# One-hot rows for expert 0, four banks for the output projection, and permuted token slots in a transformer block with a mixture of experts

## The chip, the cores and the metric

The kernel runs on one core of one Trainium2 chip. The core has five engines with an instruction queue each: TensorE (PE in the profile, with its weight loads as PEld), VectorE (DVE), ScalarE (ACT), GpSimd (POOL) and SyncE (SP, which here only issues DMAs). They share an SBUF of 128 partitions; matmul results land in eight banks of PSUM, each 128 partitions by 512 float32 numbers. Sixteen DMA engines move data between HBM and SBUF. The engines run side by side and wait for each other only by semaphores.

The metric is the device time of one execution in microseconds (us), here the median of three timed runs. Everything is float32.

## The reference, cut to what matters

```python
# 128 context tokens and 256 latent tokens, D_MODEL = 1024; N_EXPERTS = 32 in 4 groups, D_EXPERT = 256
def trunk_layer(x, mod, lp, latent, ctx_k, ctx_v, s0_fwd, s0_bwd):
    sh1, sc1, g1, sh2, sc2, g2 = jnp.split(mod, 6, axis=-1)
    h = ln_plain(x) * (1 + sc1) + sh1
    ...                                       # attention and gated linear attention from h @ w_in
    merged = gates[:, :, 0] * (attn @ lp['w_br_attn']) + gates[:, :, 1] * (gla @ lp['w_br_gla'])
    x = ln_affine(DEEPNORM_ALPHA * x + g1 * (merged @ lp['w_out']), lp['ln1_g'], lp['ln1_b'])
    h2 = ln_plain(x) * (1 + sc2) + sh2
    x = ln_affine(DEEPNORM_ALPHA * x + g2 * hier_moe(h2, lp), lp['ln2_g'], lp['ln2_b'])

def hier_moe(h, lp):
    lg = (t @ lp['router_group_w'] + lp['router_group_b'])      # the best of 4 groups
    le = (t @ lp['router_expert_w'] + lp['router_expert_b'])    # the best 2 of its 8 experts
    ...
    for e in range(N_EXPERTS):
        hid = jax.nn.silu(t @ lp['exp_w_gate'][e]) * (t @ lp['exp_w_up'][e])
        y = y + comb[:, e:e + 1] * (hid @ lp['exp_w_down'][e])
```

Each of the 384 tokens goes to 2 of the 32 experts, so 768 pairs of token and expert are computed. An expert's three weights are 1 MB each.

## The kernel before, in words

The tokens are three tiles of 128 (tiles 0 and 1 latent, tile 2 context). The program is written out by hand for each engine; PE's order of work is the order of the code. Where a result goes to a PSUM bank, a small table (`Banks`) hands out the banks of a ring in turn: `claim` makes PE wait until the last user of the bank was read, `wait_full` makes a reader wait for the matmuls, `was_read` gives it back.

The first part (to about 343 us) computes modulation, projections, both mixers and the branch projections; the change doesn't touch it, except that one group of loads is issued there. What comes then, in order:

- **Output projection** (PE L1779): for each tile and each half of the 1024 columns, 8 matmuls over 512 columns, six groups in all, that take banks 0 and 1 in turn. DVE (L1073 to the `norm_affine` calls) multiplies each half by the gate, adds the scaled residual (L1077) and takes statistics of the half (L837); with both halves it does the affine layer norm with `ln1_g` and `ln1_b` (aggregate L844, L846, L854), where GpSimd computes the power -0.5 (L689), and at once the second, modulated norm (L837, L844, L846, L851), whose last instructions write the rows `h2` of the tile and raise `h2_ready`. `ln1` is loaded by ACT (L1431) into a piece of Y that the branch outputs occupied until then.
- GpSimd stores each tile's `h2` to HBM (L727) as half rows of 2 KB, two for each token.
- **Router**: PE transposes `h2` (L1646), ACT copies the transposes (L1435), PE multiplies by the router's weights (L1796); DVE picks group and two experts (L1089 to L1121, `both_ready`). PE computes each token's rank among the tokens of its expert by triangular matmuls (L1804, L1806). Between these, `keep_busy(n)` has PE do n idle matmuls of 512 columns (L1523).
- **Index tables**: DVE picks the ranks out (L1132, L1139) and compares each with a row of constants `iota_rows` (L1147), PE multiplies the six one-hot tables (L1823), and DVE writes the indices `gidx` and `sidx` (L1151, L1152). An expert has 64 slots; column j of `iota_rows` holds the rank that slot j takes. In the kernel before that is j itself. A slot is two rows (partition j and partition 64 + j) of 2 KB, the halves of a token. Unused slots get an index out of bounds and move nothing but a few bytes.
- **Experts** (32, one after the other): GpSimd gathers an expert's rows from HBM (L732), PE transposes them (L1839), ACT copies (L1446), PE multiplies by gate and up weights (L1865, two groups of 64 output partitions side by side), ACT and DVE make the hidden values (L1464, L1188), PE transposes and multiplies by the down weights (L1898, L1874), DVE scales (L1206), GpSimd scatters to HBM (L737). Six weight buffers are filled by SP: the first ones from 315 us on, as their space comes free (down of expert 1 and all of 2 behind the last group of the output projection, 4 behind `h2_ready`, the up weights of 5 when `h2` is stored and transposed). From expert 6 on, gate and up weights are asked for when the gate and up products of the expert six before are done (`gu_full`), the first time at expert 0.
- The last two experts' rows are added by PE; the others' sums are read back from HBM (SP L664), added and normed.

SP's and ACT's loads each keep their order on one queue, GpSimd's on a third.

## Time and profile before

| | us |
|---|---|
| median of three timed runs | 677.2 (675.61 to 678.33) |
| the profiled execution's own time | 672.36 |
| its span, first to last instruction | 670.6 |
| PE busy | 621.0 (93%) |
| DVE busy | 265.9 |
| GpSimd busy | 115.6 |
| ACT busy | 106.6 |

The profiled execution is 4.8 us under the median of the timed ones. "Busy" for PE counts the time from issue to a modelled end, and the idle matmuls of `keep_busy` too. The row of digits for DMA gives the busy share of the sixteen DMA engines in 40 slices of 16.8 us: it is 9 from the 27th slice to the 38th, that is from about 436 to 637 us. The stretch before, from 352 to 436 us, is 5, 0, 9, 7, 8.

### The profile page before, as it was taken

The page shows a single profiled execution, that of the slowest core. Times are in us where ns is not written, and L with a number is a line of the kernel's source. Part 1 is how long each engine was busy: PE and PEld are TensorE (multiplying, and loading weights), DVE is VectorE, ACT ScalarE, POOL GpSimd, SP SyncE. Part 2 cuts the span into 40 slices and gives each one's busy share as a digit, 9 for nine tenths or more (in the row PEclk, how much of TensorE's full clock was granted, in tenths as well). Part 3 has the DMA queues.
Part 4 walks back from the last instruction along what each step waited for, and adds up shares of the span by engine and source line. Part 5 has one row for each costly group of instructions (what it writes and reads, how often), then busy time and mean ns, then how long its engine had stood idle before and what let it go on. Part 6 is the DMA issues. An engine that isn't in the chain of part 4 may idle for free.

```text
span 670.6 us, 8592 instructions
## 1 busy us (share of the span) xinstructions
PE 621.0 (93%) x3403; PEld 344.4 (51%) x3403; DVE 265.9 (40%) x593; ACT 106.6 (16%) x222; POOL 115.6 (17%) x114
## 2 busy tenths in 40 slices
PE   6999999999999999999999998999999887788994
PEld 3553355546455556555544464665566544444541
DVE  4322533145445544302224865334333232222347
ACT  2001553110032222330000021111111111111000
POOL 4000000010300000000001323334334222221102
PEclk9999999999999999999999999999999999988998
DMA  9998737344131130409995097899999999999862
GB/s 336 376 332 289 251 127 251 126 158 157 24 127 58 69 126 1 126 0 317 372 402 223 38 359 296 333 420 416 413 414 417 413 417 414 415 416 419 352 241 94
DMA packets 56200, 176.65 MB, mean 263 GB/s; under 512 B 10644, under 2 KB 12724, under 8 KB 44512
## 3 DMA queue, kind: packets, MB, share of 16 engines
q1 hardware_dynamic: 39264, 143.34, 55.4%
q10 hardware_dynamic: 11152, 24.47, 10.4%
q0 software_dynamic: 5744, 8.28, 3.5%
q8 instruction: 28, 0.46, 0.3%
q14 instruction: 12, 0.10, 0.0%
HBM read 174.58 MB, written 11.96 MB: 278 GB/s over the span
## 4 chain that ended last, share of the span: by engine, by line
PE 60%; DMA 22%; DVE 8%; issue 2%; POOL 2%; ACT 2%; SPq 2%; ACTq 0%; DVEq 0%; POOLq 0%
PE bank L1592 13%; PE bank L1865 11%; DMA X<-exp_w_up 8%; PE bank L1581 7%; PE bank L1766 6%; PE bank L1874 5%; DMA Y<-exp_w_up 4%; PE bank L1545 3%; DMA Y<-ln_b 3%; DMA X<-w_ada 2%; PE bank L1505 2%; DMA Y<-w_ada 2%; POOL rstd L689 2%; PE bank L1839 2%; PE bank L1733 1%
## 5 line engine op out<-in xcount | busy, mean ns | idle before, releaser
L1865 PE MATMUL bank<-X,Y 128*64 128x256 f32 x672 | 82.0, 395 | 11.8 <-DMA X<-exp_w_up 10.8
L1592 PE MATMUL bank<-Y,W 128*128 128x384 f32 x256 | 86.6, 492 | 0.0
L1865 PEld LDWEIGHTS bank<-X,Y 128*64 128x64 f32 x672 | 50.7, 137 | 48.0 <-DMA X<-exp_w_up 18.0
L689 POOL TENSOR_TENSOR rstd<-ss,cst 128x1 f32<-128x1 f32 (+3 forms) x21 | 22.6, 1075 | 295.7 <-DVE ss L822 295.7
L1592 PEld LDWEIGHTS bank<-Y,W 128*128 128x128 f32 x256 | 47.4, 190 | 36.0 <-issue 5.6
L1581 PE MATMUL bank<-W,Y 128*128 128x512 f32 x144 | 64.0, 597 | 0.0
L732 POOL DMA_INDIRECT Y<-h_rows,gidx x32 | 41.4, 1293 | 92.9 <-PE bank L1839 88.4
L1192 DVE COPY abias<-bank 128x128 f32<-128x128 f32 x32 | 9.3, 292 | 117.1 <-PE bank L1898 117.1
L1865 PE MATMUL bank<-W,Y 128*64 128x256 f32 (+1 forms) x320 | 37.2, 346 | 7.5 <-DMA W<-exp_w_up 3.9
L737 POOL DMA_INDIRECT pair_rows<-PTr,sidx x32 | 32.9, 1029 | 61.2 <-DVE PTr L1206 60.6
L1779 PE MATMUL bank<-X,Y 128*128 128x512 f32 x96 | 41.7, 594 | 1.3 <-issue 1.0
L1874 PE MATMUL bank<-X,abias 128*64 128x512 f32 x176 | 42.6, 603 | 0.0
L1581 PEld LDWEIGHTS bank<-W,Y 128*128 128x128 f32 x144 | 26.7, 190 | 30.9 <-issue 30.7
L1766 PE MATMUL bank<-Y,W 128*128 128x384 f32 x128 | 41.8, 487 | 0.8 <-PE bank L1592 0.5
L1464 ACT ACTIVATE abias<-bank 128x128 f32<-128x128 f32 x32 | 8.9, 278 | 186.9 <-PE bank L1865 180.2
L1545 PE MATMUL bank<-W,Y 128*128 128x288 f32 (+1 forms) x96 | 33.8, 504 | 0.7 <-DVE Y L919 0.7
L1865 PEld LDWEIGHTS bank<-W,Y 128*64 128x64 f32 x320 | 23.2, 139 | 20.7 <-DMA W<-exp_w_up 5.7
L1766 PEld LDWEIGHTS bank<-Y,W 128*128 128x128 f32 x128 | 24.2, 190 | 18.4 <-issue 2.0
L1206 DVE TENSOR_TENSOR PTr<-bank,abias 128x512 f32<-128x512 f32 x32 | 22.1, 692 | 25.6 <-PE bank L1874 25.6
L1779 PEld LDWEIGHTS bank<-X,Y 128*128 128x128 f32 x96 | 18.1, 190 | 24.7 <-issue 24.7
L1523 PE MATMUL bank<-cst 128*128 128x512 f32 x48 | 25.0, 660 | 5.0 <-DMA cst<-consts 5.0
L1062 DVE TENSOR_TENSOR Y<-bank,Y 128x384 f32<-128x384 f32 x16 | 8.9, 558 | 46.9 <-PE bank L1766 46.9
(232 smaller groups left out, 723.2 us busy)
## 6 DMA issues: line engine op xcount, KB each, us to landing
X<-exp_w_gate SPq DMA_DIRECT2D x22, 1024.0 KB, 22.1
X<-exp_w_up SPq DMA_DIRECT2D x22, 1024.0 KB, 26.1
X<-exp_w_down SPq DMA_DIRECT2D x22, 1024.0 KB, 26.6
Y<-w_ada ACTq DMA_DIRECT2D x16, 1024.0 KB, 8.2
W<-w_in SPq DMA_DIRECT2D x7, 2048.0 KB, 9.0
W<-exp_w_gate SPq DMA_DIRECT2D x10, 1024.0 KB, 22.1
W<-exp_w_up SPq DMA_DIRECT2D x5, 1024.0 KB, 26.7
W<-exp_w_down SPq DMA_DIRECT2D x5, 1024.0 KB, 29.7
```

Of the source, the lines that this page charges most:

```text
L689: nc.gpsimd.tensor_tensor(rstd[:, 0:n], ss[:, 0:n], const("mhalf", 0, n), ALU.pow)\
L732: pool.indirect_dma_start(G[:, n % NSLOT, :], None, h2_d, bass.IndirectOffsetOnAxis(ap=gidx[:, n:n + 1], axis=0), bounds_check=2 * TOKENS ...
L737: pool.indirect_dma_start(yp_d, bass.IndirectOffsetOnAxis(ap=sidx[:, n:n + 1], axis=0), Yo[:, n % NY, :], None, bounds_check=2 * TOPK * TO ...
L1206: V.tensor_tensor(Yo[:, n % NY, :], banks[6][:, :], gw, ALU.mult).then_inc(S["y_ready"], 1)
L1523: mm(banks[6][:, :], ident, cst[:, 0:HALF], start=True, stop=True)
L1545: ins = mm(bank[:, 0:cols], hT[:, i, k, :], w[:, k, :], start=k == 0, stop=k == KT - 1)
L1581: ins = mm(bank[:, :], hT[:, i, k, :], w[:, k, :], start=k == 0, stop=k == KT - 1)
L1592: ins = mm(bank[:, 0:TOKENS], w[:, k, c * P:(c + 1) * P], hT[:, :, k, :], start=k == 0, stop=k == KT - 1)
L1766: ins = mm(bank[:, 0:TOKENS], w[:, m, k, (c % 4) * P:(c % 4 + 1) * P], src[:, :, k, :], start=k == 0, stop=k == 3)
L1779: ins = mm(bank[:, :], mT[:, i, k, :], w[:, k, :], start=k == 0, stop=k == KT - 1)
L1865: ins = mm(bank[hh * 64:hh * 64 + 64, a:b], x_[:, c, h * 64:h * 64 + 64], rhs(hh), start=k == 0 and a == 0, stop=k == KT - 1, skip_group_c ...
L1874: ins = mm(banks[6][o * 64:o * 64 + 64, :], hT_[:, hh * 64:hh * 64 + 64], wd[hh][:, o * HALF:(o + 1) * HALF], start=hh == 0, stop=hh == 1, ...
```

## The change: what it does

1. **ln1 earlier, g2 later.** ACT loads `ln1_g` and `ln1_b` into PTr right behind the modulation rows; the four small loads of the second gate, which went there, come behind `h2_ready` of the last tile. The intermediate of the second norm goes to Y instead of PTr.
2. **Four banks, last piece halved.** The output projection takes banks 0, 1, 4 and 5 in turn, and the last group (tile 2, second half) becomes two of 256 columns; DVE handles these in two pieces, and takes tile 2's statistics in four pieces of 256 columns.
3. **Expert 0's rows by one-hot products.** DVE makes three one-hot tables of 64 slots from the rank matrix; PE multiplies them with `h2` in SBUF (6 matmuls into bank 1), ACT copies. Expert 0 is not gathered from HBM any more. The idle matmuls are 6 behind the router (5 before), 1 behind the ranks (2), and none before expert 0's transposes (4). SP's load of expert 5's up weights waits for these products in place of the last transposes.
4. **Permuted slots.** Column j of `iota_rows` holds another rank: ranks 0 to 7 go to slots 0, 4, 8, ... 28, ranks 8 to 15 to slots 1, 5, 9, ..., and so on in each block of 32 slots.

```diff
-    put("iota_rows", np.repeat((np.arange(P) % SLOT_ROWS)[None], P, 0))
+    at = np.arange(P) % SLOT_ROWS
+    put("iota_rows", np.repeat((at // 32 * 32 + at % 4 * 8 + at % 32 // 4)[None], P, 0))
...
-FILL_NORM, FILL_ROUTER, FILL_RANK, FILL_GATHER = 4, 5, 2, 4
+FILL_NORM, FILL_ROUTER, FILL_RANK = 4, 6, 1
...
+WO_COLS = {(n, i): slice(n * HALF, (n + 1) * HALF) for i in range(TILES) for n in range(2)}
+WO_COLS[1, LAST_TILE] = slice(HALF, HALF + HALF // 2)
+WO_COLS[2, LAST_TILE] = slice(HALF + HALF // 2, 2 * HALF)
...
-        ln1 = lambda j: Y1[:, j, 0, :]
-        ln2 = ln1
+        ln1 = lambda j: PTr[:, 2 * j:2 * j + 2, :].rearrange("p a n -> p (a n)")
+        ln2 = lambda j: Y1[:, j, 0, :]
...
+        last = Banks((0, 1, 4, 5), banks, full, read, last_jobs(), uses)
+        expert0 = Banks((1,), banks, full, read, [("rows",)], uses)
...
-            side.wait_full(sp, "hT", TILES - 1, 1)
+            expert0.wait_full(sp, "rows")
             load_part(sp, "exp_w_up", 1, PARTED, PARTED, ew_in[PARTED])
...
-            for n in range(NSLOT):
+            for n in range(1, NSLOT):
                 gather_rows(n)
...
+                    for c in range(cols.start, cols.stop, chunk):
+                        ins = V.bn_stats(stats[:, c // chunk, :], x1(i)[:, c:c + chunk])
+                    step(ins)
...
             bank = side.wait_full(dve, "rank")
+            for i in range(TILES):
+                ins = V.tensor_scalar(first_slots[:, i, :], const("iota_rows", 0, SLOT_ROWS), bank[:, i * NE:i * NE + 1],
+                                      both[:, i, 0:1], ALU.is_equal, ALU.mult)
+            ins.then_inc(S["onehot_ready"], FIRST_SLOTS)
...
+            bank = expert0.wait_full(act, "rows")
+            expert0.was_read(A_(G[:, 0, :], bank[:, :], ACT.Copy), "rows")
...
+            pe.wait_ge(S["onehot_ready"], FIRST_SLOTS)
+            bank = expert0.claim(pe, "rows")
+            for i in range(TILES):
+                for h in range(2):
+                    ins = mm(bank[h * SLOT_ROWS:(h + 1) * SLOT_ROWS, :], first_slots[:, i, :],
+                             xr(i)[:, h * HALF:(h + 1) * HALF], start=i == 0, stop=i == TILES - 1, skip_group_check=True)
+            expert0.filled(ins, "rows")
...
             index_tables(0)
-            keep_busy(FILL_GATHER)
             next_tokens(0)
```

VectorE, tile 2 of the output projection, from the gate's product to the last row of `h2`. Before:

```order
L1073 TENSOR_TENSOR Y<-bank,X 128x512
L1077 SCALAR_TENSOR_TENSOR Y<-Y 128x512
L837 BN_STATS stats<-Y 128x6
L1073 TENSOR_TENSOR Y<-bank,X 128x512
L1077 SCALAR_TENSOR_TENSOR Y<-Y 128x512
L837 BN_STATS stats<-Y 128x6
L844 BN_AGGR mv<-stats 128x2
```

The same place with the change:

```order
L1092 TENSOR_TENSOR Y<-bank,X 128x512
L1097 SCALAR_TENSOR_TENSOR Y<-Y 128x512
L1100 BN_STATS stats<-Y 128x6 x2
L1092 TENSOR_TENSOR Y<-bank,X 128x256
L1097 SCALAR_TENSOR_TENSOR Y<-Y 128x256
L1100 BN_STATS stats<-Y 128x6
L1092 TENSOR_TENSOR Y<-bank,X 128x256
L1097 SCALAR_TENSOR_TENSOR Y<-Y 128x256
L1100 BN_STATS stats<-Y 128x6
L862 BN_AGGR mv<-stats 128x2
```

Three instructions of 512 columns became six of 256, and there are four statistics in place of two.

TensorE, from the idle matmuls behind the router to expert 0's gate and up products. Before:

```order
L1523 MATMUL bank<-cst 128x512 x5
L1804 MATMUL bank<-both,cst 128x96
L1806 MATMUL bank<-both,cst 128x64
L1806 MATMUL bank<-both,cst 128x32
L1812 MATMUL bank<-both,cst 128x32 x3
L1523 MATMUL bank<-cst 128x512 x2
L1820 MATMUL bank<-cst 128x64
L1823 MATMUL bank<-wgate,abias 128x64 x4
L1823 MATMUL bank<-wgate,zbias 128x64 x2
L1523 MATMUL bank<-cst 128x512 x4
L1839 MATMUL bank<-cst,Y 128x128 x4
L1865 MATMUL bank<-X,Y 64x256 x16
```

With the change:

```order
L1550 MATMUL bank<-cst 128x512 x6
L1832 MATMUL bank<-both,cst 128x96
L1834 MATMUL bank<-both,cst 128x64
L1834 MATMUL bank<-both,cst 128x32
L1840 MATMUL bank<-both,cst 128x32 x3
L1550 MATMUL bank<-cst 128x512
L1851 MATMUL bank<-Y,abias 64x512 x6
L1856 MATMUL bank<-cst 128x64
L1859 MATMUL bank<-wgate,abias 128x64 x4
L1859 MATMUL bank<-wgate,zbias 128x64 x2
L1875 MATMUL bank<-cst,Y 128x128 x4
L1901 MATMUL bank<-X,Y 64x256 x16
```

The six products of expert 0's rows (L1851) stand ahead of the index tables, and the four idle matmuls behind the tables are gone.

ScalarE, its loads around the output projection. Before:

```order
L1418 DMA X<-modulation_rows 128x1024 x6
L1422 DMA PTr<-modulation_rows 64x512 x4
L1428 DMA Y<-x_sample 128x1024 x2
L1428 DMA Y<-x_prompt 128x1024
L1431 DMA Y<-ln_g 128x1024
L1431 DMA Y<-ln_b 128x1024
L1435 ACTIVATE Y<-bank 128x512 x6
L1439 DMA Y<-ln_g 128x1024
L1439 DMA Y<-ln_b 128x1024
```

With the change:

```order
L1444 DMA X<-modulation_rows 128x1024 x6
L1447 DMA PTr<-ln_g 128x1024
L1447 DMA PTr<-ln_b 128x1024
L1451 DMA Y<-x_sample 128x1024 x2
L1451 DMA Y<-x_prompt 128x1024
L1455 ACTIVATE Y<-bank 128x512 x6
L1460 DMA PTr<-modulation_rows 64x512 x4
L1464 DMA Y<-ln_g 128x1024
L1464 DMA Y<-ln_b 128x1024
```

The first pair of `ln` loads moved ahead of the `x` loads, and the four loads of the second gate moved behind the evictions.

## Rows read from the trace of the kernel before

**Rows 1.** The page's first line: span and instructions
```profile
span 670.6 us, 8592 instructions
```

**Rows 2.** Stretches: length, busy of five engines, granted clock, DMA share, GB/s
```profile
409.00:411.00 2.00, 1.40 (x13) 1.30 (x12) 0.65 (x4) 0.00 (x0) 0.00 (x0) 1.00 1.04 432
...
413.00:422.50 9.50, 7.97 (x56) 5.31 (x54) 0.52 (x2) 2.75 (x4) 6.71 (x8) 1.00 0.38 106
422.50:530.00 107.50, 106.89 (x864) 66.73 (x863) 40.52 (x91) 14.88 (x34) 39.58 (x34) 1.00 1.01 412
532.41:614.86 82.45, 67.91 (x483) 36.27 (x483) 22.60 (x50) 8.75 (x20) 21.85 (x19) 0.96 1.02 416
...
630.00:634.00 4.00, 4.00 (x19) 1.47 (x17) 2.03 (x4) 0.00 (x0) 1.26 (x1) 1.00 0.80 328
```

**Rows 3.** Timeline of PE, gate and up products of experts 18 and 28: start, length
```profile
532.41 3.84 PE L1865 MATMUL bank<-X,Y 128*64 128x256 f32 x32 [2.09 <-DMA X<-exp_w_up]
...
614.86 3.85 PE L1865 MATMUL bank<-X,Y 128*64 128x256 f32 x32
```

**Rows 4.** The chain of waits, its last part
```profile
594.08 28.50 DMA Y<-exp_w_up
```

**Rows 5.** Timeline of SP: the first load that expert 0 releases
```profile
420.90 0.33 SPq L485 DMA_DIRECT2D X<-exp_w_gate  x1
```

**Rows 6.** Timeline of DVE in the output projection
```profile
359.00 0.69 DVE L837 BATCH_NORM_STATS2 stats<-Y 128x6 f32<-128x512 f32 x1
363.02 0.21 DVE L844 BATCH_NORM_AGGREGATE mv<-stats 128x2 f32<-128x12 f32 x1 [3.33 <-DMA Y<-ln_b]
...
373.52 0.69 DVE L1073 TENSOR_TENSOR Y<-bank,X 128x512 f32<-128x512 f32 x1
...
384.01 0.69 DVE L1073 TENSOR_TENSOR Y<-bank,X 128x512 f32<-128x512 f32 x1
...
388.42 0.21 DVE L844 BATCH_NORM_AGGREGATE mv<-stats 128x2 f32<-128x12 f32 x1
...
395.28 1.41 DVE L851 SCALAR_TENSOR_TENSOR Y<-PTr,rstd,X 128x512 f32<-128x512 f32 x2 [0.52 <-POOL rstd L689]
```

**Rows 7.** Timeline of PE from the output projection to expert 0
```profile
343.43 27.71 PE L1779 MATMUL bank<-X,Y 128*128 128x512 f32 x64 [0.30 <-PE bank L1766]
372.13 13.97 PE L1779 MATMUL bank<-X,Y 128*128 128x512 f32 x32 [0.99 <-issue]
...
392.32 3.68 PE L1523 MATMUL bank<-cst 128*128 128x512 f32 x8
396.75 1.23 PE L1646 MATMUL bank<-cst,Y 128*128 128x128 f32 x8 [0.75 <-DVE Y L851]
...
400.00 4.54 PE L1523 MATMUL bank<-cst 128*128 128x512 f32 x10
405.61 0.46 PE L1804 MATMUL bank<-both,cst 128*128 128x96 f32 x2 [1.07 <-DVE both L1121]
...
409.70 1.10 PE L1823 MATMUL bank<-wgate,abias 128*128 128x64 f32 x8 [0.60 <-DVE zbias L1147]
...
415.50 0.75 PE L1839 MATMUL bank<-cst,Y 128*128 128x128 f32 x4 [0.76 <-DMA Y<-h_rows,gidx]
417.02 3.85 PE L1865 MATMUL bank<-X,Y 128*64 128x256 f32 x32 [0.78 <-ACT Y L1446]
```

**Rows 8.** Groups by form: busy, mean ns
```profile
L879 DVE TENSOR_TENSOR Y<-X,cst 128x256 f32<-128x256 f32 x4 | 1.7, 425 | 0.1
L879 DVE TENSOR_TENSOR Y<-X,cst 128x64 f32<-128x64 f32 x4 | 0.9, 226 | 0.1
```

**Rows 9.** Timeline of PE: one expert's down products, four matmuls
```profile
427.31 1.94 PE L1874 MATMUL bank<-X,abias 128*64 128x512 f32 x8
```

**Rows 10.** Timeline of GpSimd: the first gather; then the page's queue row of GpSimd's DMAs
```profile
412.34 1.11 POOL L732 DMA_INDIRECT Y<-h_rows,gidx  x1 [3.62 <-DVE sidx L1152]
...
q0 software_dynamic: 5744, 8.28, 3.5%
```

More of the change, by code:

```diff
@@ L619, in _ @@
             load_part(sp, "exp_w_gate", 0, PARTED, PARTED, ew_in[PARTED])
-            for n in range(2):
-                main.wait_full(sp, "wo", n, TILES - 1)
+            for n in range(3):
+                last.wait_full(sp, "wo", n, LAST_TILE)
             load_down(sp, 1, 1, ed_in[1])
@@ L1791, in _ @@
                 if i == 0:
-                    bank = main.claim(pe, "router")
+                    bank = last.claim(pe, "router")
                 for g in range(2):
@@ L1879, in next_tokens @@
             def next_tokens(n):
[L1880 removed]
+                if n:
+                    pe.wait_ge(g_in[n % NSLOT], (n // NSLOT + (n % NSLOT > 0)) * 16)
+                else:
+                    expert0.wait_read(pe, "rows")
                 if n:
```

87 lines of the change are left out of this document (46 added, 41 removed).

## The prediction, made before the changed kernel ran

> **What bounds the kernel now.** I read the page first, then the stretches, because PE's busy share of 93% is an average over stages with different limits. From 422.50 to 614.86 us the sixteen DMA engines are busy without a break, at a share of 1.01 to 1.02 and 412 to 416 GB/s [rows 2]. The same span of time holds the experts. In its second part PE waits for the up weights of nearly every expert [rows 3]: from 532.41 to 614.86 us lie ten experts, so 8.25 us each, while the gate and up products themselves take 3.84 us. The chain of waits ends in the same place, in a load of up weights that took 28.50 us from issue to landing, because it stood behind others [rows 4]. So the end of the kernel is set by two things: when the unbroken stream of weights starts, and how fast the slowest DMA engine works through it. Behind the last of these loads (594.08 + 28.50 = 622.6) come 48 us up to the end of the span at 670.6 [rows 1]: PE, scatter, read-back and norms, which the change leaves alone.
>
> The start of the stream is a release: the first load of it is issued at 420.90 us [rows 5], when expert 0's gate and up products (417.02 + 3.85) are done [rows 7]. From 413.00 to 422.50 us the DMA engines are busy only 0.38 of the time [rows 2]. What brings expert 0 forward closes this hole, and all that follows moves with it. Expert 0 itself hangs on a serial chain: output projection, two norms for each tile, router, ranks, tables, gather, transposes.
>
> **The change part by part.** All times are of the profiled execution.
>
> *ln1 earlier.* Tile 0's statistics end at 359.00 + 0.69 = 359.7, but the aggregate starts at 363.02, behind ln_b's landing [rows 6]. With the load issued ahead of the x loads, behind the modulation rows, that wait of 3.3 us goes. The 0.5 MB more in that earlier stretch meets w_out, which isn't needed before 343.43; I count nothing. What is late next is PE: the fourth group ends 343.43 + 27.71 = 371.1 [rows 7], so DVE takes tile 1's second half at about 371.4 in place of 373.52 [rows 6]. That is 2.1 us at this point.
>
> *Four banks, last piece halved.* With two banks PE lost 0.99 us at 372.13 waiting for a bank [rows 7]; that goes, and the last group ends near 385.0 in place of 386.1. DVE begins tile 2 at 384.01 - 2.1 = 381.9. Its work there was 388.42 - 384.01 = 4.41 us. Now the first half costs 0.69 + 0.04 + 0.69 + 0.04 and two statistics of 256 columns, each taken at 0.43 as the 256-column product of another line [rows 8], 2.3 us in all; the two quarters cost six instructions of 0.43 and a gap of 0.03, 2.8 us. The sum is 5.1, so 0.7 more than before, and it ends at 387.0. PE's last quarter is there by 385.0, so DVE never waits: the halving hides nothing any more and costs 0.7. If 256 columns cost half of 512 (0.35), the loss is 0.2; by 0.5 each it is 1.2. `h2_ready` of tile 2 comes 2.1 - 0.7 = 1.4 us sooner. PE's idle matmuls ahead of its transposes end at 396.0 - 1.0 = 395.0, against `h2` at 396.69 - 1.4 = 395.3 [rows 6, 7]: no new wait.
>
> *One more idle matmul behind the router.* Ten half matmuls took 4.54 us, twelve take 5.45; PE was idle for 1.07 us behind them [rows 7]. 0.9 fits; nothing.
>
> *The one-hot tables on DVE.* Three instructions of 64 columns ahead of the rank products, at 0.226 us [rows 8] or less: 0.65 us, all on the path to the tables, since DVE has no gap there. Two scalars, one from PSUM, could make it 1.2. Behind them wait ranks, tables, indices and the gathers for experts 1 to 3.
>
> *Expert 0's rows on PE.* Four matmuls of this shape (64 output partitions, 512 columns, the two halves of a bank in turn) took 1.94 us [rows 9], so six take 2.9 us. PE starts them after one idle matmul, 0.9 us behind the counts' last product. In us from the ranks' first product, which moves from 405.61 to 404.2: products of ranks and counts 1.4, idle matmul 0.9, rows 2.9, which gives 409.4. The tables are ready at 409.7 - 1.4 + 0.65 = 408.9, so they wait 0.5 us for PE, and the index tables end near 411.3. ACT's copy of the rows lies beside them. Transposes run at 411.3, and by the same 1.52 us as before (417.02 - 415.50 [rows 7]) gate and up start at 412.85. Before it was 417.02. **Expert 0 is 4.2 us sooner**: 1.4 from the norms, minus 0.65 for the tables, minus 0.75 for the rows that the tables wait behind (0.5, and the opening product that no longer runs early), plus 4.2 for the gather, its wait and issue (from 411.3, the tables' end before as now, to 415.50). The gather for expert 1 starts near 412.4, where the one for expert 0 did [rows 10], and lands 3.1 us later if it does as that one did, ahead of 416.7, when PE wants it. If the six products didn't run in pairs, they would cost 12 x 0.43 = 5.2 us and the gain would be 1.9; without the tables' delays at all it would be 5.5.
>
> *The stream.* The first release moves from 420.90 to 416.7. But the gathers and scatters that ran in the hole (0.38 of 9.5 us, that is 3.6 us of all engines) have only 5.3 us of it left; those of about 1.8 us fall away or still fit, one gather is gone, and some 0.7 us of work moves into the full stretch. The stream ends **3.5 us sooner** by this alone.
>
> *The slots.* A DMA can be no faster than its slowest engine. Three weights are 3.15 MB; at the 432 GB/s of a stretch with hardly anything else [rows 2] they take 7.3 us, at 420 they take 7.5, and the experts come every 8.25 us. So the engine that sets the pace spends 0.75 to 0.95 us per expert on gathers and scatters. The mean engine spends less: 8.28 MB in 3.5% of 670.6 us [rows 10] are 2.8 us per MB, and 24 tokens (768 over 32) gathered and scattered are 0.2 MB, so 0.5 us. And from 630.00 to 634.00, after the last load, the share is 0.80 [rows 2]: some engines are done and others have a backlog. That is skew, and the permutation acts on it. How rows go to engines no row tells. If neighbouring pairs of rows go to the sixteen engines in turn, the engine with the first pair always has four rows in each transfer, 8 x 0.08 = 0.64 us per expert and more for experts with over 32 tokens: near the measured excess. Counting the tokens of each expert in the reference's router (6 to 59) by this rule, with 0.16 us for a pair of rows (4 KB at 432/16 = 27 GB/s), half of it for a single row and 0.01 for none, the fullest engine has 22.9 us of gathers and scatters before and 21.1 after, as the even pairs fill with ranks 0 to 15 and the odd ones with 16 to 31. I take **1.7 us sooner** up to the last load that matters, with bounds of 0 and, for a perfect spread, 22.9 - 14.6 = 8.3.
>
> Here a rule speaks for another result. The Trainium skill, DMA: Bandwidth & Descriptors, section "Why a DMA increments its semaphore by 16 and not by 1", says that GpSimd's direct copies may give each engine a block of one sixteenth of the partitions, so 8 rows in a row. By that rule the first engine would have 71 us of small transfers before and 54 after, a rate of 8.6 us per expert before. The trace's 8.25 doesn't agree, so I give it a small chance below.
>
> **The sum.** -3.5 - 1.7 = -5.2 us. Against the profiled execution: 672.36 - 5.2 = 667.2. The median of the runs shown lies 4.8 above that execution; I carry the difference over: 677.2 - 5.2 = 672.0 us. What a measurement of this kernel can tell from no change is about 0.5%, 3.4 us.
>
> **The rivals.**
> - *Only the start moves.* The permutation changes nothing, as when the pace is set by something else than the fullest engine. -3.5: 673.7. For it: the share of 1.02 shows no idle engine; against it: 8.25 us per expert against 7.8 by the mean engine's load. Chance 0.22.
> - *The early gain is lost before the first release.* The gather for expert 1, or the load of the second gate (now behind `h2_ready`, sharing the engines with 7 MB of weights), comes late and expert 0 or 1 stands; or the six products don't pair. The first release gains 1 to 2 us: 675.5. Chance 0.14.
> - *Blocks of eight rows.* The rule above: 17 us less on the fullest engine, of which the release order gives back part, as PE then sets the pace in many experts: I take about half, and the earlier start with it, -11, so 666. Chance 0.06.
> - *Slower: single rows go to engines in turn.* Then slots 0, 4, 8, ... hit four engines only. The place is the stream from expert 6 on. With 0.08 us a row the fullest engine goes from 37.4 to 44.3 us: +6.9 - 3.5 = +3.4, so 680.6. It decides once the four engines' extra rows exceed what the earlier start gave, 3.5 us. For it: the same skew of sixteen us between engines. Against it: 37.4 us over 28.5 experts (27 gathers and 30 scatters) are 1.3 us per expert, more than the excess of 0.95. Chance 0.06.
> - The forecast has the rest, 0.52, with its own range of 669.5 to 674.
>
> **How the numbers follow.** Faster by over 0.5% means under 673.8: nine tenths of the forecast (0.47), half of the first rival (0.11), all of the third (0.06), 0.64. Slower by over 0.5%: the fourth rival's half and a little of the second and of the scatter between runs, 0.06. The rest, 0.30, is within 0.5%. The range reaches from between the forecast and the third rival, 668.3, to 676.5, which holds the first and most of the second.
>
> **What would show it.** In the changed profile: no wait for ln at the first aggregate, which starts near 359.7; tile 2's `h2` near 395.2; the six products in about 2.9 us; expert 0's gate and up near 412.9 and SP's first refill near 416.7; the DMA share full from about 418 on; 8.15 to 8.2 us per expert in the second part; the last waited load landing near 617.4. The forecast is wrong if the first refill isn't at least 3 us sooner, or if it is and the last waited load isn't.

## The result, and the profile of the changed kernel

The changed kernel took 664.07 us (median of 4 executions, 663.80 to 667.03) against 676.52 (675.61 to 678.33) on the same chip: a ratio of 0.9826, with a 95% interval of 0.9806 to 0.9845. That is 12.5 us less; 5.2 less were forecast, and 664.07 lies below the range. Two more series of runs gave 665.33 and 664.64 for the same kernel (ratios 0.9863 [0.9839, 0.9886] and 0.983 [0.9809, 0.9852]). The median of all 15 executions is 664.64, and that is the changed kernel's time below where a kernel of another series is compared with it. The series ran on different chips: the kernel before took 676.9 us beside experiments 1 to 4, 675.5 beside 5 to 8, 674.5 beside 9 to 14 and 676.1 beside 15 and 16. So a difference of medians from two series carries up to some 2.5 us; the ratios, each against the kernel before in its own series, and the landings in the traces are the better measures.

The profiled execution is the longest of its four, 667.03 us. The page's span, TensorE clock, DMA shares and GpSimd queue, to be read against [rows 1, 10]:

```profile
span 665.3 us, 8643 instructions
...
PEclk9999999999999999999999999999999999999898
DMA  9997737345030330308995089999999999999952
...
q0 software_dynamic: 5664, 8.14, 3.5%
```

The first digit 8 near the end of the clock's row is a fall to half clock (1.2 GHz in place of 2.4) at 618.7 us, which the other three executions don't show in their time (spans of 662.0 to 662.4).

The output projection and the norms on DVE (start us, length, instruction, idle time before it in brackets), which answer to [rows 6]:

```profile
360.17 0.21 DVE L862 BATCH_NORM_AGGREGATE mv<-stats 128x2 f32<-128x12 f32 x1
...
371.72 0.69 DVE L1092 TENSOR_TENSOR Y<-bank,X 128x512 f32<-128x512 f32 x1 [1.10 <-PE bank L1807]
...
382.21 0.69 DVE L1092 TENSOR_TENSOR Y<-bank,X 128x512 f32<-128x512 f32 x1
...
384.45 0.42 DVE L1092 TENSOR_TENSOR Y<-bank,X 128x256 f32<-128x256 f32 x1
...
387.20 0.27 DVE L862 BATCH_NORM_AGGREGATE mv<-stats 128x2 f32<-128x24 f32 x1
...
394.13 1.41 DVE L869 SCALAR_TENSOR_TENSOR Y<-Y,rstd,X 128x512 f32<-128x512 f32 x2 [0.52 <-POOL rstd L706]
...
405.62 0.77 DVE L1154 TENSOR_SCALAR abias<-cst,bank,both 128x64 f32<-128x64 f32 x3
```

The wait for ln_b is gone, PE is next (1.10 us), and the three one-hot tables take 0.77. On PE, from the idle matmuls to the second expert, against [rows 7]:

```profile
405.81 1.10 PE L1550 MATMUL bank<-cst 128*128 128x512 f32 x2
...
409.84 1.06 PE L1859 MATMUL bank<-wgate,abias 128*128 128x64 f32 x8
...
411.18 0.68 PE L1875 MATMUL bank<-cst,Y 128*128 128x128 f32 x4
412.64 3.85 PE L1901 MATMUL bank<-X,Y 128*64 128x256 f32 x32 [0.78 <-ACT Y L1471]
416.78 0.75 PE L1875 MATMUL bank<-cst,Y 128*128 128x128 f32 x4 [0.29 <-DMA Y<-h_rows,gidx]
```

Expert 0 no longer waits for a gather; expert 1 does, for 0.29 us. Its gather was issued at 412.43, so it was used 4.3 us behind its issue. The stretches (length, busy time of five engines, granted clock, DMA share, GB/s) and the last load in the chain of waits, against [rows 2, 4]:

```profile
413.00:417.00 4.00, 3.71 (x33) 2.51 (x30) 0.60 (x3) 1.01 (x2) 3.08 (x4) 1.00 0.72 258
...
526.80:606.84 80.04, 64.73 (x483) 34.88 (x483) 23.27 (x50) 8.75 (x20) 22.34 (x19) 1.00 1.02 416
```

```profile
586.47 28.04 DMA Y<-exp_w_up
```

From 526.80 to 606.84 lie ten experts that wait for up weights: 8.00 us each, against 8.25. The last waited load lands at 586.47 + 28.04 = 614.5, against 622.6: 8.1 us sooner, of which expert 0's earlier start (412.64 against 417.02) explains at most 4.4. The first load that expert 0 releases is issued at 416.79, against 420.90 in [rows 5]. From there to the last waited landing it is 197.7 us, against 201.7 before.

### The profile page after: what moved, and what is told of

Same layout as the page of the kernel before. It is cut to its first block, busy times and chain, and to the rows that moved or that the text cites. A ratio compares the mean times of both kernels' runs of the same rounds, so it can differ in the third digit from the quotient of the medians.

```text
span 665.3 us, 8643 instructions
## 1 busy us (share of the span) xinstructions
PE 619.1 (93%) x3423; PEld 348.1 (52%) x3423; DVE 266.9 (40%) x600; ACT 107.2 (16%) x223; POOL 114.5 (17%) x113
## 4 chain that ended last, share of the span: by engine, by line
PE 70%; DMA 15%; DVE 8%; issue 3%; ACT 2%; POOL 1%; SPq 0%; ACTq 0%; DVEq 0%; POOLq 0%
PE bank L1619 13%; PE bank L1901 12%; PE bank L1608 7%; PE bank L1793 6%; PE bank L1910 5%; DMA Y<-exp_w_up 4%; PE bank L1807 4%; DMA X<-exp_w_up 4%; DMA W<-exp_w_up 4%; PE bank L1572 3%; PE bank L1532 2%; DMA Y<-w_ada 2%; PE bank L1875 2%; POOL rstd L706 1%; PE bank L1760 1%
## 5 line engine op out<-in xcount | busy, mean ns | idle before, releaser
L1901 PE MATMUL bank<-X,Y 128*64 128x256 f32 x672 | 80.6, 389 | 12.4 <-DMA X<-exp_w_up 11.4
L706 POOL TENSOR_TENSOR rstd<-ss,cst 128x1 f32<-128x1 f32 (+3 forms) x21 | 22.6, 1074 | 294.4 <-DVE ss L839 294.4
L1807 PE MATMUL bank<-X,Y 128*128 128x512 f32 (+1 forms) x112 | 41.5, 532 | 0.3 <-PE bank L1793 0.3
L1901 PEld LDWEIGHTS bank<-W,Y 128*64 128x64 f32 x320 | 24.6, 139 | 19.3 <-issue 5.5
L1807 PEld LDWEIGHTS bank<-X,Y 128*128 128x128 f32 x112 | 21.2, 190 | 20.8 <-issue 20.0
L1550 PE MATMUL bank<-cst 128*128 128x512 f32 x40 | 22.0, 691 | 5.0 <-DMA cst<-consts 5.0
```

The source lines that it names most:

```text
L706: nc.gpsimd.tensor_tensor(rstd[:, 0:n], ss[:, 0:n], const("mhalf", 0, n), ALU.pow)\
L1550: mm(banks[6][:, :], ident, cst[:, 0:HALF], start=True, stop=True)
L1807: ins = mm(bank[:, 0:width], mT[:, i, k, :], w[:, k, at:at + width], start=k == 0, stop=k == KT - 1)
L1901: ins = mm(bank[hh * 64:hh * 64 + 64, a:b], x_[:, c, h * 64:h * 64 + 64], rhs(hh), start=k == 0 and a == 0, stop=k == KT - 1, skip_group_c ...
```

## The experiments

Below, "lands" is the landing of that last load in the kernel's own profile, counted from the start of its output projection (between 342.5 and 344.2 us). So 614.5 - 343.9 = 270.6 for the changed kernel and 622.6 - 343.4 = 279.2 for the first profile of the kernel before. The two other profiles of the changed kernel (experiments 9 and 16) both give 270.4, so the landing repeats far better than a median does. The "first refill" is the first load that expert 0 releases. The theory that the experiments test was formed from the two traces: **an indirect DMA of 64 slots (128 partitions, two halves of a row) gives four neighbouring slots to one of eight DMA engines in turn; the second halves go to the other eight; and the fullest engine paces the stream.** The trace doesn't name the engine of a packet, but its order shows through: a packet holds two neighbouring rows, and each engine closes its part with a packet of 4 bytes (16 of them in each gather). Expert 0 has 35 tokens. Its gather in the kernel before has 34 packets of two rows, 2 of one row and 28 of none, and each of the two one-row packets (slot 34, in either half) is followed directly by such a closing packet. So slot 34 stands last on its engine, behind slots 0 to 3, which the theory says and the turn of the prediction doesn't.

With 0.16 us for two rows in one packet, 0.085 for one row and 0.009 for none, all from the packets in the traces, and the tokens of each expert from the reference's router, the fullest engine's gathers (experts 5 to 31) and scatters (0 to 29) come to 22.6 us before and 16.4 us after, the mean engine's to 14.6.

**1. The slots alone, on the kernel before.**

```
# at = np.arange(P) % SLOT_ROWS
- iota_rows = at
+ iota_rows = at // 32 * 32 + at % 4 * 8 + at % 32 // 4
```

> The kernel before with the permuted slots alone. Theory A (found in the changed trace): the rows of a gather or scatter go to the DMA engines in runs of four neighbouring slots, one run to each of eight engines in turn, the second half rows to the other eight. By this the fullest engine's small transfers fall from 22.6 to 16.4 us, so experts come every 8.0 us in place of 8.25, the last up weights that PE waits for land about 6 us sooner with the first refill unmoved, and the time is 5 to 7 us less. Rival B (my prediction: neighbouring pairs to sixteen engines in turn): 1.7 us less. Rival C: the permutation does nothing and the time is that of before.

672.34 us (670.94 to 674.43), ratio 0.9935 [0.9914, 0.9957]. Lands at 278.9. From expert 0's gate and up to that landing it took 202.3 us, against 207.2 in experiment 3; from the first refill (425.52) it took 196.8, against 201.7 in both profiles of the kernel before. So the slots alone take 4.9 us off the stream. The time is 4.6 us less than the kernel before beside it (676.9). Expert 0 came late here, which hid part of the gain in the landing:

```profile
418.53 0.75 PE L1840 MATMUL bank<-cst,Y 128*128 128x128 f32 x4 [2.78 <-DMA Y<-h_rows,gidx]
420.05 4.31 PE L1866 MATMUL bank<-X,Y 128*64 128x256 f32 x22 [0.78 <-ACT Y L1447]
```

PE stood 2.78 us for the gather (0.76 in [rows 7]), and the clock fell to half at 420.2 us, while the products ran. The first packet of the gather moved 1.8 us behind its issue, as in [rows 10]'s gather, but one DMA engine still worked through packets of SP's loads, 0.31 us each, until 417.7. The wait for the gather isn't the fixed 0.76 us that I took from one execution.

**2. The changed kernel with the old slots.** The same edit, the other way round.

> The changed kernel with the slots in their old order. Theory A: it loses 5 to 7 of the 12.5 us gained, so about 670 us against 676.5 before; expert 0 stays at about 412.6 and experts come every 8.25 us. Rival B: it loses 1.7 us, about 666. Rival C: 664.

671.22 us (669.30 to 672.60), ratio 0.9915 [0.9894, 0.9937]. Expert 0 starts at 412.29, lands at 276.4. **The slots are worth about 6 us in the changed kernel:** 276.4 - 270.6 = 5.8 by the landings, 671.2 - 664.6 = 6.6 by medians of different series, 3.5 to 6.0 by the ratios of the three series of the changed kernel. The map gives 6.2, the prediction 1.7. The other edits together are worth 676.9 - 671.2 = 5.7 us, measured side by side, where 3.5 were forecast.

**3. The kernel before again.**

> The kernel before, once more, for a second profile and the spans and clocks of more executions. Theory K (clock): the 4 us between the profiled execution of before (672.36) and its timed ones (675.6 to 678.3) are falls of the granted clock at places where PE sets the pace, so the spans go with the mean granted clock and with the place of the falls; a profile with a longer span shows one between the last awaited weights and the end. Rival: the front part or the stream of weights varies, and the last awaited load lands later in a longer execution.

676.96 us in the middle of 12 executions, ratio 0.9996 [0.9982, 1.0011]; one of them came at 3546.88, and without it the median is 676.92 (674.66 to 678.55). It gives a second profile of the kernel before, at 675.53 us:

```profile
416.16 0.74 PE L1839 MATMUL bank<-cst,Y 128*128 128x128 f32 x4 [0.76 <-DMA Y<-h_rows,gidx]
417.68 3.84 PE L1865 MATMUL bank<-X,Y 128*64 128x256 f32 x32 [0.78 <-ACT Y L1446]
```

```profile
596.33 28.54 DMA Y<-exp_w_up
```

It lands at 281.4, 2.2 us behind the profile of the prediction. Those 2.2 us are there at the start of the stream already: the first refill is issued at 423.12, against 420.90, and from it to the landing both executions take 201.7, to within 0.1. Of the delay 0.7 us is expert 0's own start. The rest is that the refill comes 1.6 us behind the end of expert 0's products (417.68 + 3.84), where it came directly behind them in [rows 5]; what held it the trace doesn't say. The clock doesn't explain it, as it doesn't fall before 668.8 here.

**4. The changed kernel with expert 0 gathered.** The three one-hot tables, the six products and ACT's copy are gone. The first gather is back, and the idle matmuls are four ahead of its rows, five behind the router and two behind the counts. SP's load of expert 5's up weights waits for the last transposes again.

```
- for n in range(1, NSLOT):
+ for n in range(NSLOT):
      gather_rows(n)
```

> The changed kernel with expert 0 gathered from HBM as before (no one-hot tables, products and copy; idle matmuls 5, 2 and 4 as before), all else as changed. By the sum of the prediction expert 0's gate and up start at 417.02 - 1.4 = 415.6 in place of 412.6, and the stream's start moves by the same 3 us, so 2.5 to 3 us more than the changed kernel: about 666.8. Rival: the hole in the stream is filled by other transfers and the start is worth nothing: 664.

672.06 us (670.70 to 673.98), ratio 0.9931 [0.991, 0.9952]; lands at 277.4. GpSimd's issue of the gather and PE's wait:

```profile
410.83 1.11 POOL L749 DMA_INDIRECT Y<-h_rows,gidx  x1 [3.62 <-DVE sidx L1174]
```

```profile
416.77 1.13 PE L1862 MATMUL bank<-cst,Y 128*128 128x128 f32 x4 [3.54 <-DMA Y<-h_rows,gidx]
418.68 2.40 PE L1888 MATMUL bank<-X,Y 128*64 128x256 f32 x10 [0.78 <-issue]
```

```profile
410.00:413.00 3.00, 3.00 (x8) 1.14 (x6) 1.78 (x11) 0.00 (x0) 1.86 (x2) 1.00 1.03 408
413.00:416.00 3.00, 0.23 (x1) 0.00 (x0) 0.00 (x0) 0.00 (x0) 2.27 (x3) 0.96 0.95 369
416.00:419.00 3.00, 1.45 (x6) 1.06 (x8) 0.00 (x0) 1.04 (x2) 2.21 (x3) 0.50 0.38 130
```

The gather is issued 1.5 us sooner than before, since the norms are sooner, and used 5.9 us later: the sixteen engines are busy until about 416 (in the kernel before until about 412). The first packet of the gather moves at 414.5, 3.6 us behind its issue (1.8 in the kernel before), and from there the gather shares the engines with the norm's loads and the next gathers. Part of this backlog is the change's own: the four loads of the second gate (0.5 MB) are issued here from 396.6 us on, ahead of the last norm's two loads, where the kernel before issued them at 305; no run takes these four apart. Nothing is left of the earlier norms, and the clock fell to half at 415.7, while PE stood idle. So one-hot rows are worth 672.1 - 664.6 = 7.5 us beside this gather (6.8 by the landings, 6.2 by the mean ratio), where I had 2.8 us of expert 0's start. Experiments 10 and 11 take it apart.

**5. The changed kernel with the old output projection:** two banks, last piece whole, ln rows behind the merged tiles, the expert gates' rows (0.5 MB) early.

```
- last = Banks((0, 1, 4, 5), ...)
+ last = Banks((0, 1), ...)
```

> The changed kernel with the output projection, its banks and the ln loads as before (two banks, whole halves, ln1 behind the merge, second gate early); one-hot rows and permuted slots stay. By the prediction's sum `h2` of the last tile and expert 0 come 1.4 us later than in the changed kernel (about 414.0 in place of 412.6), and the end with them: 665.5 against 664.1. Rival (the bank and ln edits are worth nothing, as the pair of gather0 and perm_only, 672.1 and 672.3, suggests): 664.1.

667.75 us (665.68 to 668.73), ratio 0.9881 [0.986, 0.9902]: 3.1 us above the changed kernel by medians of different series. In the profile expert 0 starts 71.0 us behind the output projection's start, not 68.8, and it lands at 272.6, 2.0 us later. So these edits bring expert 0 forward by 2.2 us, where the prediction had 1.4. The first aggregate waits again:

```profile
362.98 0.21 DVE L860 BATCH_NORM_AGGREGATE mv<-stats 128x2 f32<-128x12 f32 x1 [4.02 <-DMA Y<-ln_b]
```

**6. The last piece whole again, the rest as changed.**

```
- WO_COLS[1, LAST_TILE] = slice(HALF, HALF + HALF // 2)
- WO_COLS[2, LAST_TILE] = slice(HALF + HALF // 2, 2 * HALF)
```

> The changed kernel with four banks but the last group whole. Prediction on record: halving costs 0.7 us of DVE and hides nothing, so without it 663.4. Rival (from the changed trace): without the halving DVE would have to wait for the whole last group, which ends near 385.3, and the aggregate would start near 387.5 in place of 387.2, so 0 to 0.4 us later: 664.3.

666.15 us (664.09 to 672.31), ratio 0.9876 [0.9838, 0.9913]; this doesn't stand apart from the changed kernel in time. The profile does tell:

```profile
381.85 0.69 DVE L1090 TENSOR_TENSOR Y<-bank,X 128x512 f32<-128x512 f32 x1
...
385.10 0.69 DVE L1090 TENSOR_TENSOR Y<-bank,X 128x512 f32<-128x512 f32 x1 [1.10 <-PE bank L1805]
...
387.28 0.21 DVE L860 BATCH_NORM_AGGREGATE mv<-stats 128x2 f32<-128x12 f32 x1
```

Without the halving DVE waits 1.10 us for PE's last half. Tile 2 takes 387.28 - 381.85 = 5.43 us, with it 387.20 - 382.21 = 4.99. The halving gains 0.44, and expert 0 starts 69.1 us behind the output projection's start in this profile, against 68.8.

**7. The slots in snake order:** every second run of eight ranks is dealt backwards.

```
+ turn = np.where(at % 2 == 0, at % 32 // 4, 7 - at % 32 // 4)
- iota_rows = at // 32 * 32 + at % 4 * 8 + at % 32 // 4
+ iota_rows = at // 32 * 32 + at % 4 * 8 + turn
```

> The changed kernel with another order of the slots: ranks 8 to 15 and 24 to 31 of a block run through the eight runs of four slots backwards. Theory A (four neighbouring slots to one of eight engines for each half row): the fullest engine's small transfers go from 16.4 to 14.8 us, so the last awaited load lands 1.2 to 1.7 us sooner and the time is about 662.6. Rival B (neighbouring pairs to sixteen engines): no gain, 664.1.

663.63 us (663.52 to 664.65), ratio 0.9824 [0.9801, 0.9848]; lands at 270.3 against 270.6. The map promised 1.6 us less on the fullest engine; what is there is not more than the scatter. From first refill to landing it takes 197.7 us in both.

**8. The old slots, and every scatter twice,** the second to a spare tensor.

```
  scatter_rows(m, scattered[m % NY])
+ scatter_rows(m, scattered[m % NY], spare_d)
```

> The changed kernel with the slots in their old order (e2_no_perm, 671.2 us) and every scatter of experts 0 to 29 issued a second time, into a spare tensor that nobody reads. Theory A: the fullest engine gets 11.5 us more and sets the pace, so 681 to 683, and experts come every 8.6 us. Rival (the mean over the engines counts): 7.5 us more, 678.7. Rival (gathers and scatters fit beside the weights): 671.

683.71 us (682.94 to 684.84), ratio 1.0115 [1.0093, 1.0136]: 12.5 us more than experiment 2 by the medians, 13.5 by the ratios. That is 1.0 us or 2.0 above the 11.5 of the fullest engine's share, and 5.0 or 6.0 above the 7.5 of the mean engine's. The clock fell to half seven times between 510 and 625 us in this profile, and not once there in experiment 2; but PE waited for the up weights of every expert from 527 us on (0.40 to 2.60 us), so the stream still set the pace.

**9 and 16. The changed kernel again.**

> The changed kernel once more, as the measure for the other kernels of this set and for the ones before it (old output projection 667.75, last piece unhalved 666.15, snake order 663.63). If those differences are real, 664.1 +- 1; if the set of the output projection gives nothing, this one comes at 666 to 667. The clock's fall in the tail, seen in the profiled execution at 667.03, should be in few executions: the median keeps to 664.

> The changed kernel itself on the same chip, unchanged. 664.07 and 665.33 were its medians so far, with 3 of 10 executions over 666: again 664 to 665.5, highest 667 to 669.

665.33 us (663.44 to 668.60) and 664.64 (663.59 to 666.55). Both lie nearer to experiments 6, 7 and 12 than I had read from the first median.

**10. Expert 0 gathered, with ten idle matmuls for four** ahead of its tokens.

```
- FILL_GATHER = 4
+ FILL_GATHER = 10
```

> The changed kernel with expert 0 gathered again (672.06 measured), and ten idle matmuls in place of four between the index tables and expert 0's tokens, so PE is busy until the gather has landed (about 417) instead of idle for 3.5 us. Theory: of the 8.0 us that the one-hot rows are worth, the part that isn't the gather's landing is PE's idle time, behind which the granted clock falls to half while expert 0's products run (5.64 instead of 3.85 us). Then expert 0's gate and up start at 418.7 to 419.2 and take 3.85, the second at 424.5 to 425, and the time is 670.3 +- 0.8. Rival (the clock falls for another reason, or the stream doesn't care): 672 +- 0.7.

671.12 us (669.79 to 671.55), ratio 0.9938 [0.9921, 0.9956]. Expert 0's products now run at full clock, in 3.85 us and not 5.64, but start at 420.55 in place of 418.68; the second expert starts at 426.26 against 426.19. Of the later start 0.9 us isn't the idle matmuls': in this execution the clock fell to half at 405.9, ahead of the index tables, and the ten matmuls began at 410.50 and not at 409.58. They took 8.80 us, as 20 halves, and cost the other 1.0. The time is unchanged against experiment 4 by the ratios (0.9938 and 0.9931), so the run bounds the clock's part at the 1.8 us by which the products were longer, and no more; my start was some 1.5 us too early.

**11. Expert 0 gathered, and the last norm's two loads (1 MB) issued at the start of the output projection.** The intermediate of the second norm goes to another tile to make room.

```
  for t in range(TILES): act.dma_start(xr(t), src)...
+ act.wait_ge(S["merged_ready"], KT)
+ for j in range(2): act.dma_start(ln2(j), ...)
```

> The changed kernel with expert 0 gathered, and the two loads of the last norm (1 MB) issued before the output projection instead of behind the last h2. Theory: expert 0's gather lands behind what the other queues have left over from the stretch 386 to 416 us; with 1 MB less of it (2.4 us at 415 GB/s) it lands at 414 to 415 in place of about 416.8, PE idles 1 to 2 us instead of 3.5, expert 0's gate and up start at 416 to 417, and the time is 669.5 +- 1. Rival (the gather's own latency is 5 us whatever stands before it): 672 +- 0.7, or 671.5 by the stream's megabyte alone if anything moves out of the full stretch.

**666.56 us** (665.48 to 667.43), ratio 0.9871 [0.9851, 0.9891]: 5.5 us less than experiment 4 by the medians, 4.1 by the ratios and 4.8 by the landings (272.6 against 277.4), for two loads that nobody waits for until the end. The gather, PE's wait and the stretches:

```profile
411.10 1.11 POOL L749 DMA_INDIRECT Y<-h_rows,gidx  x1 [3.24 <-DVE sidx L1174]
```

```profile
414.19 0.75 PE L1863 MATMUL bank<-cst,Y 128*128 128x128 f32 x4 [0.71 <-DMA Y<-h_rows,gidx]
415.72 3.85 PE L1889 MATMUL bank<-X,Y 128*64 128x256 f32 x32 [0.78 <-ACT Y L1468]
```

```profile
410.00:413.00 3.00, 3.00 (x8) 1.23 (x7) 2.00 (x12) 0.00 (x0) 1.60 (x2) 1.00 0.61 243
413.00:416.00 3.00, 1.52 (x9) 0.81 (x9) 0.00 (x0) 1.00 (x2) 2.39 (x3) 1.00 0.44 127
```

Most engines are free from about 412, and the gather is used 3.1 us behind its issue instead of 5.9. The rival, a fixed latency of 5 us, falls. With this order of loads the one-hot rows would be worth 272.6 - 270.6 = 2.0 us by the landings; beside the changed kernel in the same series (665.33) it is 1.2 us, which the intervals don't tell from nothing.

**12. The changed kernel with the snake order, the same early loads, and no idle matmul between counts and rows.**

> The changed kernel with three edits: snake order of the slots, the last norm's loads early, and no idle matmul between counts and rows. The snake order takes the fullest engine's small transfers from 16.4 to 14.8 us by the map of four neighbouring slots to one engine (measured alone: 663.63 against 664.07); the idle matmul gone starts expert 0's rows sooner by up to 0.9 us, of which the tables let through 0.4; the loads' megabyte is no longer in the hole and makes room for the refills: up to 1 us. Expected 662.3 +- 0.8. Rival (PE or the first gathers already set the start of the stream, and the rest is the weights' own time): 663.6 +- 0.6.

665.75 us (663.87 to 669.90), ratio 0.9864 [0.9835, 0.9892]; lands at 271.3. A miss: no gain. Once expert 0 doesn't wait for a gather, the loads' backlog holds nobody up, and expert 0 starts 69.3 us behind the output projection's start, not sooner than 68.8. Without the idle matmul PE stood 1.41 us for the one-hot tables instead.

**13. The slots crowded.** Ranks 0 to 3 on slots 0 to 3, ranks 4 to 7 on slots 32 to 35, and so on.

```
- iota_rows = at // 32 * 32 + at % 4 * 8 + at % 32 // 4
+ iota_rows = at % 32 // 4 * 8 + at // 32 * 4 + at % 4
```

> The changed kernel with the slots in a third order, worse than the old one if a run of four neighbouring slots goes to one of eight engines in turn and slots 32 to 63 begin with the same engine again: ranks 0 to 3 on slots 0 to 3, ranks 4 to 7 on slots 32 to 35, ranks 8 to 11 on slots 4 to 7, and so on, so that one engine gets eight ranks in a row. By that map the fullest engine's gathers and scatters come to 35.7 us, against 22.6 in the old order and 16.4 in the permuted one; the mean engine stays at 14.6. Theory (the fullest engine paces the stream): 13.1 us more than the old order's 671.2 where every expert waits for weights, some of it hidden in the experts that PE sets: 681 to 685. Rival (no gain or loss beyond the spread over pairs, as the prediction had it: what counts is full, half and empty pairs on sixteen engines): this order has the same pairs on the same engines as one in which each pair stands twice, 22 to 30 us, 672 to 678. Rival (the mean engine counts): 664 to 665, as the changed kernel.

680.96 us (679.67 to 681.62), ratio 1.0094 [1.0065, 1.0122]. Its last load, then those of the old slots (experiment 2) and the snake order:

```profile
602.17 29.73 DMA Y<-exp_w_up
```

```profile
591.42 28.51 DMA Y<-exp_w_up
```

```profile
586.06 27.79 DMA Y<-exp_w_up
```

| slots | fullest engine by the map | lands | first refill to landing | time | ratio |
|---|---|---|---|---|---|
| snake (7) | 14.8 | 270.3 | 197.7 | 663.6 | 0.982 |
| changed | 16.4 | 270.6 | 197.7 | 664.6 | 0.983 to 0.986 |
| old (2) | 22.6 | 276.4 | 203.5 | 671.2 | 0.992 |
| crowded (13) | 35.7 | 288.3 | 215.7 | 681.0 | 1.009 |

The same rows and bytes, 17 us apart. In the crowded order's profile the clock fell to half six times between 510 and 610 us, but PE waited for the up weights of every expert from 502 to 632 us (0.53 to 2.47 us), so the stream set the pace there too. From old to crowded the landing moves by 11.9 us for 13.1 on the fullest engine, from old to changed by 5.8 for 6.2. Under 16 us nothing more comes. The crowded order doesn't speak against the prediction's turn of pairs over sixteen engines: with the same counts and prices that rule gives 36.5 us for it, not the 22 to 30 expected above. What that rule can't give is the step from old to changed, 1.8 us by it, and the order of packets in the first gather.

**14 and 15. Three idle matmuls of 128 columns ahead of the gate and up products of experts 14 to 28,** in snake order (14) and in the changed kernel's order (15).

```
  def next_gate_up(n):
+     for _ in range(3 if 14 <= n <= CHECK else 0):
+         mm(banks[7][:, 0:P], ident, ident, start=True, stop=True)
```

> The changed kernel in snake order (663.63 alone), with three idle matmuls of 128 columns (0.8 us) ahead of the gate and up products of experts 14 to 28. PE is busy for 6.5 us of each expert's 8.0 there, so they fit into its wait for the up weights. Theory: executions differ by 1 to 5 us because the granted clock falls to half for 3.4 us in some of them, at places between 500 and 625 us where PE waits for weights; with less idle time in that stretch the falls stay away and the spread narrows: 663.3 +- 0.7, highest of six under 665.5. Rival (the falls come from something else, or at other places, such as the experts after 28): spread as before, 664 to 666 with a highest of 667 to 670. Second rival: the matmuls delay the down products and the slots' release, 665 to 668.

> The changed kernel, in its own order of the slots, with the three idle matmuls ahead of the gate and up products of experts 14 to 28 that narrowed the snake order's kernel to 662.83 to 663.92. If the idle matmuls keep the clock up in this stretch: median 663.5 to 664.5 and no execution over 666. If the narrow spread there was the snake order's, or chance: 664 to 665.5 with a highest of 667 to 670, as the kernel beside it.

14: **663.13 us** (662.83 to 663.92), ratio 0.9834 [0.9812, 0.9856], the lowest median of all, though its ratio is no better than the changed kernel's in its own series. 15: 664.81 (664.36 to 667.74), ratio 0.9836 [0.9816, 0.9856], beside 664.64 for the kernel without them. The profiled execution of 15 was the one at 667.74, and its clock fell to half at 608.8 us, 1.9 us behind the last of these matmuls, with PE waiting for weights. So they gain nothing that I can show. Of the scatter between executions the profiles show this much: those of the changed kernel (667.03), of 12 (667.09), 15 (667.74) and 16 (666.55) have such a fall between 608 and 620 us, those of 6, 7, 9 and 14 (662.8 to 664.7) have none there. What brings it on stays open.

## Why the prediction was wrong

**Right.** The start of the stream, nearly to the digit: expert 0's gate and up forecast for 412.85, measured 412.64; the first refill for 416.7, measured 416.79. On the way there: tile 0's aggregate at 359.7 (360.17), PE next in line, tile 2's piece 5.1 us (4.99), tables on DVE 0.65 (0.77), the six products 2.9 (2.79, so they do run in pairs). Expert 1's gather was in time but for 0.29 us, and that with some luck: it was used 4.3 us behind its issue, not the 3.1 that I carried over. That the time would follow two things, when the stream starts and how fast its slowest engine is, held too.

**Wrong, and the larger part: the term for the slots.** "If neighbouring pairs of rows go to the sixteen engines in turn" was a guess, since no row told how rows go to engines, and I took its 1.7 us as the value. Undoing the slots costs about 6 us (experiment 2: 5.8 by the landings, 6.6 by the medians), and giving them to the kernel before takes 4.9 off its stream (experiment 1). The mechanism was right, skew on the fullest engine; its size was off because the real turn is four slots, over eight engines. I had the number that should have moved me: 0.75 to 0.95 us per expert on the pacing engine against 0.5 on the mean one, over thirty experts, is 7.5 to 13.5 us of skew, and my rule left 6.5 of the 8.3 us between before and a perfect spread in place without any row for it. The bound of 8.3 was sound and the range should have reached to it: 677.2 - 3.5 - 8.3 = 665.4. Even that end would have missed 664.07 by 1.3 us, by the start's worth below. The share after the last load showed the effect as well, and it is to be compared with 0.92, 0.80, 0.59 and 0.34 in four stretches of 4 us before. After the change:

```profile
626.00:630.00 4.00, 4.00 (x23) 1.86 (x24) 2.56 (x5) 0.00 (x0) 1.44 (x1) 1.00 0.99 415
630.00:634.00 4.00, 3.31 (x30) 1.95 (x27) 0.46 (x2) 0.77 (x2) 0.98 (x1) 1.00 0.79 328
634.00:638.00 4.00, 4.00 (x35) 2.10 (x36) 2.13 (x4) 0.00 (x0) 0.00 (x0) 1.00 0.06 21
```

The engines stop within some 5 us of each other instead of 16.

**Wrong, the smaller part: the start's worth.** The forecast gave it 3.5 us; experiment 2 has 5.7. The step that failed is the one that carried the 4.8 us between the profiled execution and the median over to the changed kernel, as if they lay evenly in both. They don't: in the second profile of the kernel before (experiment 3) expert 0 is 0.7 us later and the first refill 2.2 us later, and in experiment 1 expert 0 is 3.0 us later, 1.0 us of it by later tables and 2.0 by the gather. In the three profiles of the changed kernel expert 0 starts 68.8 us behind the output projection's start each time. How the rest of the 4.8 us is made up stays open.

The discount for small transfers pushed into the full stretch was too small, 0.7 us, and this hid part of the miss. From experiment 3 to experiment 2, counted from the output projection's start, the first refill moves by 6.7 us and the landing by 5.0. From the first profile of the kernel before to experiment 2 it is 4.5 and 2.8. So 1.7 to 1.8 us go to the longer way from first refill to landing, 203.5 against 201.7. With the new slots it is 1.0: 197.7 with the early start (changed kernel) and 196.7 with a late one (experiments 4 and 11).

**A step whose total was right and whose reason was not:** "the halving hides nothing any more and costs 0.7". I compared DVE's work with and without the halving, but not PE's end without it. With the whole piece DVE waits 1.10 us for it (experiment 6). The cost of 0.58 us in tile 2 (4.99 against 4.41) is real; the wait that it saves is larger.

**The rivals.** "Only the start moves" falls by experiments 1 and 2. "The early gain is lost" is not seen in the changed kernel; it is what happens when expert 0 is gathered (experiment 4). "Single rows in turn" falls by its sign, as by it the new slots cost time. But its sum was wrong: with the same counts, 0.08 us a row and 0.005 for an empty one, the fullest engine goes from 18.8 to 22.2 us, half of the 37.4 and 44.3 recorded, so the argument that 37.4 is too much for the measured excess doesn't hold either. "Blocks of eight rows" came nearest with 666, by luck and by a wrong sum. It goes by the Trainium skill, DMA: Bandwidth & Descriptors, section "Why a DMA increments its semaphore by 16 and not by 1": some of GpSimd's direct copies give each engine one sixteenth of the partitions, in one block. Blocks of eight of the 128 partitions put 35.7 us on the fullest engine before and 26.8 after; the 71 and 54 recorded are what comes out if both halves of a token fall to the same engine, and 71 us wouldn't give the recorded 8.6 us per expert either. So the rival would have had 9 us less on the fullest engine, not 17. It falls too: by it the crowded order, whose first eight slots hold eight low ranks as the old one's do, would cost no more than the old one (33.9 us on the fullest engine against 35.7). The crowded order costs 9.7 us more by the medians, 12.1 by the ratios and 11.9 by the landings. The Trainium skill says this of direct copies; these runs show that it doesn't carry over to the indirect ones here, and the measurement decides.

## What to carry to other kernels

When the engines of a DMA are unevenly loaded and the map from rows to engines isn't known, take the bounds as the answer, nothing and the perfect spread, and read the skew from rows (the pacing engine's surplus, the way the shares fade after the last load) instead of picking a map. A single profiled execution can be a short one: compare it with the median, and ask where in the kernel the difference lies before adding a forecast to it. A small transfer on the critical path can be held up by what other queues have issued before it: look for megabytes that nobody needs yet, and issue them in an earlier idle stretch, as the two loads of experiment 11 did for 4 to 5.5 us. And for any piece that is split, work out the counterfactual on both engines.

## What the hardware showed unexpectedly

- An indirect DMA's rows go to the engines in runs of four slots over eight engines, the second 64 partitions to the other eight; the order of the slots alone moved this kernel from 663.6 to 681.0 us. The map is inferred from the order of packet sizes in the traces, which don't name the engine; four orders and the doubled scatter bear it out.
- The same gather was used 3.1 us behind its issue with free engines and 5.9 us with a backlog (experiments 11 and 4).
- The clock fell to half inside an idle stretch of PE of 3.5 us (experiment 4, at 415.7) and 1.7 us behind one of 2.8 (experiment 1, at 420.2). It also fell without such a stretch: in experiment 10 at 405.9 us, where PE had been 8.4 of the 10 us from 395 to 405 busy.
